# Stick-breaking's sums in one-pass products of high and low parts, and a new order around the fourth block's first half

## The reference, cut to what matters

```python
u, vv, q, k, v = jnp.split(proj, ...)
yc = spatial_gating(gelu(u), gelu(vv), sgu_v_norm[i], sgu_w[i], sgu_b[i])
yd = stick_breaking_attention(q.reshape(hs), k.reshape(hs), v.reshape(hs))
h = h + jnp.einsum('bse,ed->bsd', jnp.concatenate([yc, yd], axis=-1), w_out_odd[i])
...
# spatial_gating: u * (W_s rms_norm(vv) + b), in blocks of 128 positions
# stick_breaking_attention, for each head:
z = q @ k.T * inv
log_rest = jnp.where(causal, log_sigmoid(-z), 0.0)
tail = lax.cumsum(log_rest, axis=3, reverse=True) - log_rest
a = jnp.where(causal, jnp.exp(log_sigmoid(z) + tail), 0.0)
out = a @ v
```

## Time and profile before

| | |
|---|---|
| median of 3 runs | 603.98 us (601.09, 603.98, 609.18) |
| profiled execution | 608.75 us |
| its span | 607.0 us |
| granted TensorE clock, mean | 0.957 |
| busy: PE, DVE, ACT | 546.9, 178.7, 172.3 us |
| moved by DMA | 236.14 MB, mean 389 GB/s |
| mixer of layer 1, on TensorE | about 304.4 to 401.5 us of the span |
| experts of layer 1 | about 410 us to the end |

### The profile page before, as it was taken

The page is one execution under the profiler, slowest core; times in us unless marked ns, Lnnn a source line. Parts: engine busy times, 40 slices in busy tenths (PEclk is TensorE's granted clock), DMA queues, the critical chain, the costliest instruction groups (busy, mean ns, idle before and its releaser), DMA issues.

```text
span 607.0 us, 7989 instructions
## 1 busy us (share of the span) xinstructions
PE 546.9 (90%) x3338; PEld 301.7 (50%) x3338; DVE 178.7 (29%) x306; ACT 172.3 (28%) x307; POOL 6.5 (1%) x16
## 2 busy tenths in 40 slices
PE   5999899999999998668799999999999999987766
PEld 4888687444424441312288878774444344423111
DVE  3686944311101110100374465353111011101001
ACT  4845734111111110000384777341111111100100
POOL 0000000000000000000000000000000000000000
PEclk7999999999999998988799999999999999997877
DMA  8999999899999999999999955598999999999992
GB/s 307 423 420 418 422 419 421 313 425 419 421 421 419 421 421 422 421 419 419 421 419 419 422 211 205 220 423 319 425 421 420 418 421 422 421 419 421 417 419 109
DMA packets 33565, 236.14 MB, mean 389 GB/s; under 512 B 3760, under 2 KB 3760, under 8 KB 5488
## 3 DMA queue, kind: packets, MB, share of 16 engines
q1 hardware_dynamic: 32800, 232.07, 93.0%
q0 software_dynamic: 720, 3.45, 1.4%
HBM read 234.45 MB, written 1.05 MB: 388 GB/s over the span
## 4 chain that ended last, share of the span: by engine, by line
PE 65%; DMA 28%; DVE 3%; ACT 1%; issue 1%; SPq 1%; DVEq 0%; ACTq 0%
PE psum L1263 18%; DMA raw<-stream 18%; DMA late<-stream 9%; PE psum L262 8%; PE psum L263 8%; PE psum L264 8%; PE psum L1240 7%; PE psum L1311 7%; DMA xT<-x_turned 1%; PE psum L519 1%; PE psum L1325 1%; PE psum L336 1%; ACT hid L1384 1%; PE psum L1090 1%; SPq L209 1%
## 5 line engine op out<-in xcount | busy, mean ns | idle before, releaser
L1263 PE MATMUL psum<-raw,x 128*32 128x512 f32 x680 | 91.7, 641 | 22.0 <-DMA raw<-stream 11.8
L254 DVE TENSOR_TENSOR raw_lo<-raw,whi 128x1024 fp32r<-128x1024 f32 x52 | 62.5, 1222 | 47.9 <-ACT whi L247 47.7
L1311 PE MATMUL psum<-y,pickT 128*128 128x512 f32 x128 | 69.5, 668 | 4.5 <-ACT y L1390 3.5
L1240 PEld LDWEIGHTS psum<-pick,h 128*128 128x128 f32 x512 | 59.4, 193 | 18.4 <-issue 15.9
L247 ACT CAST whi<-raw 128x1024 fp32r<-128x1024 f32 x52 | 53.5, 1048 | 48.2 <-PE psum L264 41.3
L1240 PE MATMUL psum<-pick,h 128*128 128x128 f32 x512 | 63.6, 281 | 1.2 <-DVE pick L1207 1.0
L262 PE MATMUL psum<-whi,hnT_hi 128*128 128x512 f32 x144 | 58.1, 403 | 5.4 <-DVE hnT_lo L366 5.2
L1215 DVE TENSOR_TENSOR pick<-pick,lists 128x256 f32<-128x256 f32 x16 | 6.8, 424 | 178.1 <-PE psum L1325 178.1
L263 PE MATMUL psum<-whi,hnT_lo 128*128 128x512 f32 x144 | 57.8, 401 | 0.0
L264 PE MATMUL psum<-raw_lo,hnT_hi 128*128 128x512 f32 x144 | 57.4, 398 | 0.0
L1263 PE MATMUL psum<-raw,hid 128*32 128x512 f32 x376 | 48.8, 619 | 5.9 <-ACT hid L1384 5.1
(11 more groups left out here) (203 smaller groups left out, 493.3 us busy)
## 6 DMA issues: line engine op xcount, KB each, us to landing
raw<-stream SPq DMA_DIRECT2D x157, 1024.0 KB, 26.5
late<-stream SPq DMA_DIRECT2D x60, 1024.0 KB, 24.2
raw<-stream SPq DMA_DIRECT2D x2, 512.0 KB, 7.5
xT<-x_turned SPq DMA_DIRECT2D x2, 512.0 KB, 8.4
h<-x SPq DMA_DIRECT2D x1, 1024.0 KB, 12.3
pb<-even_bias POOLq DMA_DIRECT2D x1, 1024.0 KB, 13.9
pool_c<-even_pool POOLq DMA_DIRECT2D x1, 1024.0 KB, 9.4
pb<-even_bias POOLq DMA_DIRECT2D x1, 512.0 KB, 8.3
```

What stands on the lines that cost most here:

```text
L254: nc.vector.tensor_tensor(raw_lo[PLACE[c][0]][:, cols], chunk(c)[:, cols], whi[:, n % SPLIT, cols].bitcast(F32), ALU.subtract).then_inc(lo ...
L1240: mm = nc.tensor.matmul(psum[:, gather_banks(q)[part], kk * P:(kk + 1) * P], h[:, t, k * P:(k + 1) * P], pick[:, t, :], start=(t == 0), st ...
L1263: nc.tensor.matmul(psum[rows, b, :], lhs[:, rows], chunk(c)[:, e * W4:(e + 1) * W4], start=start, stop=stop).then_inc(moe_used, 1)
L1311: nc.tensor.matmul(bank(b), pickT[:, t * P:(t + 1) * P], y[:], start=(q == 0), stop=(q == QUADS - 1)).then_inc(m.scattered, 1)
```

## The change

The softplus of a group is split: ScalarE copies it rounded to fp32r (`stick_hi_act`), VectorE forms the rest (`stick_lo_dve`), and `sum_pe` makes twelve one-pass products with fp32r constants `tri` and `ones` instead of six float32 products. `ones` is a new constant, made by VectorE beside `tri`. The low part lies where `stick` lies; the high part of group 0 where group 1's `stick` will lie, and that of group 1 over the high parts of the normed input, for which ScalarE waits until all ten projection chunks are used. On TensorE `gating_pe` moves behind the first chunk of block v. On ScalarE the split of PROJ1+9 moves behind the first exponential, and the Gelu table is loaded explicitly ahead of the split of PROJ1+8. On VectorE the split of PROJ1+8 moves ahead of the norm of vv.

```diff
@@ -756,15 +756,19 @@
         HALF = 4 * S + 4 * P
 
         stick = [at("stick0", [P, 2, HALF // 2], 36.25), at("stick1", [P, 2, HALF // 2], 42.25)]
+
+        stick_hi = [at("stick_hi0", [P, 2, HALF // 2], 42.25, F32R), at("stick_hi1", [P, 2, HALF // 2], 0, F32R)]
+        stick_lo = [at("stick_lo0", [P, 2, HALF // 2], 36.25, F32R), at("stick_lo1", [P, 2, HALF // 2], 42.25, F32R)]
         vgain = at("vgain", [P, W4], 34.0625)
 
         sgu = at("sgu", [P, 4 * P + 4], 32)
         bigid, tri = at("bigid", [P, P], 48.25, F32R), at("tri", [P, P], 48.75, F32R)
+        ones = at("ones", [P, P], 49.25, F32R)
         ssv, rmsv, rsv = stat[:, 16:18], stat[:, 18:20], stat[:, 20:22]
         od = sems("odd", "sgu_landed", "vgain_landed", "ssv_ready", "rmsv_ready", "vn_ready", "gated", "yc_ready",
                   "yc_turned", "mixC_hi_ready", "mixC_lo_ready", "qk_turned", "qT_ready", "z_done", "abs_ready",
                   "exp_ready", "ln_ready", "rest_ready", "sum_done", "stick_ready", "av_done", "mixD_hi_ready",
-                  "mixD_lo_ready", "big_ready", "tril_ready")
+                  "mixD_lo_ready", "big_ready", "tril_ready", "stick_hi_ready", "stick_lo_ready")
 
         def odd_pool_loads(pool):
             pool.wait_ge(moe_used, EACH * (PER_QUAD * SPILL_AT + 1))
@@ -823,12 +827,18 @@
         def sum_pe(pe, group):
 
             z0, z1 = half_parts(z_banks)
-            r0, r1 = half_parts(stick[group][:])
-            pe.wait_ge(od.rest_ready, group + 1)
-            for par in range(2):
-                nc.tensor.matmul(z0[:, par], negtri, r0[:, par], start=False, stop=False, skip_group_check=True)
-                nc.tensor.matmul(z0[:, par, :, P:S], negones, r1[:, par], start=False, stop=True, skip_group_check=True)
-                mm = nc.tensor.matmul(z1[:, par], negtri, r1[:, par], start=False, stop=True, skip_group_check=True)
+            pe.wait_ge(od.stick_lo_ready, group + 1)
+            if group == 0:
+                pe.wait_ge(od.big_ready, 3)
+
+            for half in (stick_hi, stick_lo):
+                r0, r1 = half_parts(half[group][:])
+                last = half is stick_lo
+                for par in range(2):
+                    nc.tensor.matmul(z0[:, par], tri[:], r0[:, par], start=False, stop=False, skip_group_check=True)
+                    nc.tensor.matmul(z1[:, par], tri[:], r1[:, par], start=False, stop=last, skip_group_check=True)
+                    mm = nc.tensor.matmul(z0[:, par, :, P:S], ones[:], r1[:, par], start=False, stop=last,
+                                          skip_group_check=True)
             mm.then_inc(od.sum_done, 1)
 
         def av_pe(pe, group):
@@ -867,8 +877,8 @@
             odd_block(2, (1,), (1,))
             odd_block(3)
             sum_pe(pe, 0)
+            odd_block(4, (0,))
             gating_pe(pe)
-            odd_block(4, (0,))
             pe.wait_ge(od.stick_ready, 1)
             z_pe(pe, 1)
             pe.wait_ge(od.yc_ready, 4)
@@ -904,6 +914,18 @@
             dve.wait_ge(od.ln_ready, group + 1)
             nc.vector.scalar_tensor_tensor(stick[group][:], z_banks, 0.0, stick[group][:], ALU.max, ALU.add
                                            ).then_inc(od.rest_ready, 1)
+
+        def stick_hi_act(act, group):
+            act.wait_ge(od.rest_ready, group + 1)
+            if group == 1:
+
+                act.wait_ge(w_used, 2 * mixer_no(OUT1))
+            nc.scalar.copy(stick_hi[group][:], stick[group][:]).then_inc(od.stick_hi_ready, 1)
+
+        def stick_lo_dve(dve, group):
+            dve.wait_ge(od.stick_hi_ready, group + 1)
+            nc.vector.tensor_tensor(stick_lo[group][:], stick[group][:], stick_hi[group][:].bitcast(F32), ALU.subtract
+                                    ).then_inc(od.stick_lo_ready, 1)
 
         def weights_act(act, group):
             if group == 0:
@@ -940,17 +962,20 @@
             split_hi(act, PROJ1 + 6)
             stick_act(act, 0, lambda: split_hi(act, PROJ1 + 7))
             block_out(act, 1, PROJ1, 2, vv_in, ACT.Gelu)
+            stick_hi_act(act, 0)
             act.wait_ge(od.ssv_ready, 2)
             nc.scalar.activation(rmsv, ssv, ACT.Sqrt, bias=eps, scale=1.0 / W4).then_inc(od.rmsv_ready, 1)
+            nc.scalar.preload_act_table(ACT.Gelu)
             split_hi(act, PROJ1 + 8)
-            split_hi(act, PROJ1 + 9)
             block_out(act, 1, PROJ1, 3, u_in, ACT.Gelu)
             weights_act(act, 0)
+            split_hi(act, PROJ1 + 9)
             split_hi(act, OUT1)
             act.wait_ge(od.yc_turned, T)
             for t in range(T):
                 nc.scalar.copy(mixC_hi[:, :, t * P:(t + 1) * P], pairs_view(2 + t)).then_inc(od.mixC_hi_ready, 1)
             stick_act(act, 1)
+            stick_hi_act(act, 1)
             split_hi(act, OUT1 + 1)
             block_out(act, 1, PROJ1, 4, v1_in)
             split_hi(act, OUT1 + 2)
@@ -969,6 +994,7 @@
             rstd_dve(dve, 2)
             nc.vector.tensor_scalar(bigid[:], ident, -NEG, None, ALU.mult).then_inc(od.big_ready, 1)
             nc.vector.tensor_copy(tri[:], negtri).then_inc(od.big_ready, 1)
+            nc.vector.tensor_copy(ones[:], negones).then_inc(od.big_ready, 1)
             for c in range(PROJ1 + 2, PROJ1 + 6):
                 split_lo(dve, c)
             for t in range(T):
@@ -985,13 +1011,14 @@
             for t in range(T):
                 nc.vector.tensor_tensor_reduce(u_in[:, t, :], vv_in[:, t, :], vv_in[:, t, :], 1.0, 0.0,
                                                ALU.mult, ALU.add, ssv[:, t:t + 1]).then_inc(od.ssv_ready, 1)
+            stick_lo_dve(dve, 0)
+            split_lo(dve, PROJ1 + 8)
             dve.wait_ge(od.rmsv_ready, 1)
             link(nc.vector.reciprocal(rsv, rmsv))
             dve.wait_ge(od.vgain_landed, 16)
             for t in range(T):
                 nc.vector.scalar_tensor_tensor(vv_in[:, t, :], vv_in[:, t, :], rsv[:, t:t + 1], vgain[:],
                                                ALU.mult, ALU.mult).then_inc(od.vn_ready, 1)
-            split_lo(dve, PROJ1 + 8)
             split_lo(dve, PROJ1 + 9)
             dve.wait_ge(proj_out[1], 8)
             for g in range(4):
@@ -1007,6 +1034,7 @@
                                         mixC_hi[:, :, t * P:(t + 1) * P].bitcast(F32), ALU.subtract
                                         ).then_inc(od.mixC_lo_ready, 1)
             stick_dve(dve, 1)
+            stick_lo_dve(dve, 1)
             split_lo(dve, OUT1 + 1)
             split_lo(dve, OUT1 + 2)
             mixD_dve(dve, 0)
```

## The result

The changed kernel takes 601.67 us (median of 22 executions, 597.74 to 606.56), the one before 605.0 (22 executions, 601.09 to 609.18). The ratio is 0.9947, with a 95% interval of 0.9921 to 0.9972: 3.2 us less, with 1.7 to 4.8 inside the interval. The forecast was 600.8 against 603.98, which is 3.2 less, or a ratio of 0.9947. That the two ratios agree to the fourth place is luck: the interval would have let the gain be anything from 1.7 to 4.8 us.

A forecast was written before the change was run, and what follows sets the result against it. The weight stream was taken as the bound, its last standstill following TensorE's path through layer 1's mixer. Terms -1.52 - 1.52 - 0.54 + 0.4 = -3.2 us take the median 603.98 to 600.8 us (chance 0.62), range 597 to 606.

The forecast's parts named there:

- The bound: Weight stream bounds the kernel; a microsecond off layer 1's mixer path, TensorE's, moves its last standstill and the end one microsecond.
- The sums: Layer 1's mixer: a group's products take 1.92 us instead of 3.44, 1.52 less; at the long products' price 0.56 less.
- The gating's wait: TensorE in layer 1's mixer: the 0.54 us wait before the gating, put down to u's output, goes.
- The new wait: TensorE before block v's first chunk waits 0.4 us for PROJ1+8's split, VectorE's half ready last.
- The second group: Group 1 gives its whole 1.52 us: no wait at its sum, 0.36 to spare, and 0.3 to spare at `av_pe`.
- The sum: Mixer's end: -1.52 - 1.52 - 0.54 + 0.4 = -3.2 us; bounds -1.7 and -3.6.
- At nothing: Making `ones` on VectorE, 0.22 us, costs nothing because VectorE waited 0.52 for ScalarE right behind it.
- The table loads: ScalarE between high part and PROJ1+8's split: two loads of 1.28 us each, taken without the skill's drain of about 1.38.
- the rival built on it: ScalarE's table switches cost twice the length, 2.8 us, leaving 0.4 of the gain: 603.6 us; chance 0.02.
- ScalarE as the path: Rival in the mixer: late ScalarE steps cost 0.5 to 1.4 us per group, about 602.8 us; chance 0.15.
- a stream that stands fast: Rival: the stream's last standstill does not follow the mixer, so the end stays at 604.0 us; chance 0.06.
- The tail's clock: Rival: tail behind the last chunk runs at 1.2 GHz, losing 4.7 us, giving 605.5 us; chance 0.15.

The follow-up runs named there:

- third experiment: Changed kernel plus 12 one-pass products by zeros of 512 columns behind each group's sums: median 605.74 us, ratio 1.0012 to the kernel before.
- first experiment: One-pass sums with high and low parts, but the three engine orders of the kernel before: 606.98 us, ratio 1.0037 to the kernel before.
- second experiment: The change's new orders with the float32 sums of the kernel before, no high and low parts: median 603.92 us, ratio 0.999 to the kernel before.
- fifth: One-pass sums in the old orders, plus 12 products by zeros behind group 0's sum to fill TensorE's wait: ratio 1.0001 to the kernel before.
- sixth experiment: Changed kernel with ScalarE's high-part pass of group 1 made twice: median 604.32 us, ratio 0.9985 to the kernel before.
- fourth experiment: Changed kernel with ScalarE's split of PROJ1+8 moved ahead of the root and its two table loads: median 600.15 us, ratio 0.9929 to the kernel before.

## Why the prediction was right

**The bound.** A microsecond on this mixer's path is one at the end: shown by the third experiment (4.9 in the stretch, 4.1 in the median), and by the table, in which seven kernels follow their stretch within their intervals. These intervals are some 2 to 4 us to either side, so the closer evidence is in the traces: from the issue of chunk 147 to the first product of the last gate-and-up chunk it took 172.6 to 173.2 us before, after and in the first, second, fifth and sixth experiments, while the stretch ahead of it went from 57.7 to 63.4. In the fourth it took 171.9, which these rows do not explain; in the third TensorE was behind the stream by then and took the last three chunks without a wait.

**The sums.** 1.86 us a group for the 1.92 taken, so one sum gave 1.58 for the 1.52. The upper bound, that changing constants makes short products as dear as long ones, did not come true.

**The gating's wait.** I put it down to u's output though the profile said "issue". The second experiment shows it gone with the order alone (0.61 us less in the stretch for the 0.54), and the first shows it grown to 3.11 us when the sum ended sooner and u came later.

**The new wait.** 0.42 us idle for the 0.4, with the releaser that I named. The fourth experiment, which takes away only this, removes it, and shows that it cost the path 0.64. This term was too small by a quarter of a microsecond.

**The second group.** No wait at the second sum: 363.88 to 375.85 is 11.97 for +12.0, and the low part was ready at 373.76 + 1.76 = 375.52, 0.33 ahead. The exponential was done at 380.02, 0.57 ahead of `av_pe`, where I had 0.3. The sixth experiment shows that these margins are real and narrow.

**The sum.** 3.17 us in the stretch for 3.2, and 3.2 by the ratio. That the terms add up so closely is in part luck: the wait that cost 0.24 more than taken is made up for by 0.06 to 0.10 in each of the others. The transposes came at +11.98 from the first sum in place of +13.52, 1.54 earlier for my 1.66; the second group gave 0.03 up to its sum and 1.59 from there to `av_pe`, for my 1.52. From `av_pe` to chunk 147 it took 29.05 us before and 29.04 after.

**At nothing.** `ones` took its 0.22 us, and VectorE still waited 0.38 for ScalarE behind it.

**The table loads.** Two loads of 1.28 us stand between the high part and the split, and root and split start 0.01 to 0.02 us behind them. The Trainium skill's drain of 1.38 us besides each load (ScalarE: Activation LUTs, section What ACT_TABLE_LOAD costs) does not show in these rows; the measurement decides, and the rival built on it did not occur.

**The other rivals.** ScalarE as the path and a stream that stands fast did not occur. The tail's clock is real: it separates the two profiled executions by 3.4 us. But it is not seen as a price of this change: it hit the profile before far more than the one after, and over 22 executions of each the ratio leaves no more than the mixer's 3.2, though its interval would hide 1.5 us. The executions of either kernel spread over 8 to 9 us. How much of that is the tail is not shown, and it is not all: where the code ahead of the first sum is the same, that sum alone starts up to 6 us apart (348.31 and 354.37).

**What I missed.** The prediction priced a wait on TensorE at its length: "TensorE waits by what is missing and no more". An idle time of 0.42 us cost 0.64, one of 1.06 cost 1.4 (the sixth experiment), and one of 3.1 cost about 6, half of it in slow products. Had the order left that wait standing, the forecast would have had the wrong sign, as the first experiment's had (-0.2 expected, +2.2 measured).

## What to carry to other kernels

Cheaper products help only if the engines that feed them keep ahead: write down for each wait on the path who is ahead and by how much, and reorder together with the saving. Price an idle time of TensorE at more than its length: here the short ones cost 0.2 to 0.35 us on top, and behind the one of 3.1 us what followed ran at half the clock. And where two single profiles are compared, cut out a stretch that begins and ends at the edited work, since the rest of the span carries other differences.

## What the runs showed of the hardware

Behind 3.11 us idle TensorE ran at a granted clock of 0.50 (eight instructions in 3.75 us for 1.9); with products by zeros in that time it ran at 1.00. Behind 0.42 or 1.06 us idle the first product went 0.08 to 0.10 us more than its usual distance and the next ones went at it. Where the kernel branches on a loaded flag TensorE was idle for 3.9 to 5.6 us in each layer of every profile without products ahead of it (5.60 in the changed kernel's layer 1). The profile calls this "issue". Products of 3.9 us put ahead of it left 3.23 and 2.88 us of it, and the time was no shorter. One-pass products of 256 columns with a new constant each went 0.11 to 0.12 us apart, though each loads its 128 x 128 constant (rows of 0.19 us, which overlap the products).
